# Two expert teams and one overflow team woven step by step, with gathers of 384 columns, in a two-block model on one core

## The reference

```python
def hierarchical_moe(h, w_group, b_group, w_router, b_router, w1, w3, w2):
    ...
    top_v, top_i = lax.top_k(e_in_group, TOP_K)
    top_w = jax.nn.softmax(top_v, axis=-1) * g_w
    ...
    hid = jax.nn.silu(jnp.einsum('td,edf->tef', t, w1)) * jnp.einsum('td,edf->tef', t, w3)
    y = jnp.einsum('tef,efd->td', hid * gates.astype(hid.dtype)[:, :, None], w2)
```

## Time and profile before

| | us |
|---|---|
| median of three runs | 3269.16 |
| lowest and highest run | 3265.61, 3270.73 |
| the profiled execution | 3263.18 |
| its span | 3261.4 |

### The profile page before, as it was taken

One profiled execution on the slowest core, in us unless ns is written; L12 is line 12 of the kernel. 1 busy time (PEld: TensorE's weight loads), 2 busy tenths in 40 slices (PEclk: granted clock), 3 DMA queues, 4 the chain that ended last, 5 costly groups with the idle time before them and its releaser, 6 DMA issues.

```text
span 3261.4 us, 51720 instructions
## 1 busy us (share of the span) xinstructions
PE 2918.5 (89%) x20048; PEld 2413.4 (74%) x20048; DVE 1270.4 (39%) x2025; ACT 1183.5 (36%) x1378; POOL 1677.4 (51%) x1274
## 2 busy tenths in 40 slices
PE   6899979999899999857788768979999999999998
PEld 1677767787898878733344427879988989999998
DVE  1477742214363252331222214436633153324335
ACT  1222233333445332310111104546554446654343
POOL 0000047677677676400000003966669997769798
PEclk8999989999999999978999988989999999999999
DMA  9533337558344586659777893543335554445444
GB/s 390 205 109 109 109 112 287 199 217 296 133 151 158 182 305 249 223 209 414 328 321 314 333 420 148 191 140 138 132 131 193 182 195 155 154 142 193 158 168 142
DMA packets 98628, 679.77 MB, mean 208 GB/s; under 512 B 11584, under 2 KB 15424, under 8 KB 16832
## 3 DMA queue, kind: packets, MB, share of 16 engines
q1 hardware_dynamic: 83088, 602.97, 49.4%
q10 hardware_dynamic: 15408, 74.85, 6.1%
...
## 4 chain that ended last, share of the span: by engine, by line
PE 70%; DMA 12%; DVE 6%; ACT 5%; issue 3%; POOL 2%; ACTq 1%; SPq 1%; DVEq 0%; POOLq 0%
PE acc L567 42%; PE wk L567 11%; PE acc L640 9%; DMA ring<-in_moe 6%; PE acc L644 5%; DMA side_buf<-in_ada 3%; POOL w_lo L549 2%; DMA stage<-in_ada 2%; PE acc L653 2%; ACT L1287 1%; ACT w_hi L1287 1%; DVE C_z L1846 1%; DMA stage<-in_main 1%; SPq L499 1%; ACT hb L1287 0%
## 5 line engine op out<-in xcount | busy, mean ns | idle before, releaser
L549 POOL TENSOR_TENSOR w_lo<-stage,w_hi 128x512 fp32r<-128x512 f32 x1268 | 1670.2, 1351 | 1535.3 <-ACT w_hi L1287 1014.3
L1287 ACT ACTIVATE w_hi<-stage 128x2048 fp32r<-128x2048 f32 x317 | 603.8, 1907 | 47.9 <-DMA stage<-in_main 47.5
L567 PE MATMUL acc<-xhl,w_hi 128*128 128x256 f32 x4064 | 525.2, 288 | 21.9 <-DVE xhl L1843 9.8
L567 PEld LDWEIGHTS acc<-xhl,w_hi 128*128 128x128 f32 x4064 | 509.2, 196 | 25.9 <-DVE xhl L1843 6.8
L640 PE MATMUL acc<-xhl,w_hi 128*128 128x512 f32 x1536 | 371.3, 394 | 0.0
L640 PEld LDWEIGHTS acc<-xhl,w_hi 128*128 128x128 f32 x1536 | 281.6, 188 | 92.7 <-issue 37.7
L567 PE MATMUL acc<-xhl,w_lo 128*128 128x256 f32 x2032 | 274.6, 289 | 2.0 <-POOL w_lo L549 2.0
L567 PEld LDWEIGHTS acc<-xhl,w_lo 128*128 128x128 f32 x2032 | 259.3, 196 | 5.5 <-issue 2.5
L567 PE MATMUL acc<-h,stage 128*128 128x256 f32 x1024 | 232.8, 384 | 2.9 <-ACT h L1287 2.9
L567 PEld LDWEIGHTS acc<-h,stage 128*128 128x128 f32 x1024 | 193.5, 191 | 38.3 <-issue 12.8
L567 PE MATMUL acc<-ring,xg 128*32 128x512 f32 x1024 | 145.2, 712 | 73.0 <-DMA ring<-in_moe 72.3
...
## 6 DMA issues: line engine op xcount, KB each, us to landing
...
ring<-in_moe SPq DMA_DIRECT2D x192, 1024.0 KB, 10.4
...
```

Source lines behind the costliest of these rows:

```text
L549: last = pool.tensor_tensor(w_lo[:, k % 2, cs], stage[:, k, cs], w_hi[:, k, cs].bitcast(F32), ALU.subtract)
L567: return pe.matmul(o, w, r, start=start, stop=stop)
L1287: return act.activation(o, i, f, **kw)
```

## The change

The teams now come in four rounds of three: two real teams `a` and `b`, and one overflow team `o`. The loop over `p` gives way to a list that is the same in each round, in which each real step is followed by at most one or two pieces that take nothing from the ring: an overflow step, a combine, half a gather. The combines of `b` and `o` and the down steps of `o` move into the up steps of the next round's `a`. The chunks' order in `EXPERT` follows: `a` 0 to 3, `b` 0, `a` 4 and 5, `b` 1 to 5. There are four passes of `gather` with 384 columns, for three teams each, in place of six with 256; each but the first is done in two halves. The overflow team's picked tokens have a buffer of their own, `xgo`, so ScalarE empties each PSUM tile by two operations. `pg` and `pk2` move to other addresses. The numbers of matmuls per step, the bytes, and all that lies outside of the expert stage stay as they were.

```diff
-TEAM_ORDER = [0, 1, 2, 8, 3, 9, 4, 10, 5, 11, 6, 7]
+TEAM_ORDER = [0, 1, 8, 2, 3, 9, 4, 5, 10, 6, 7, 11]
...
-    for p, team in enumerate(TEAMS):
-        yield from ((tile, c) for c in range(4) for tile in team)
-        if p and p - 1 not in OVER_TEAMS:
-            yield from ((tile, c) for c in (4, 5) for tile in TEAMS[p - 1])
-        if p in OVER_TEAMS:
-            yield from ((tile, c) for c in (4, 5) for tile in team)
-    yield from ((tile, c) for c in (4, 5) for tile in TEAMS[-1])
+    for d in range(TRIPLES):
+        a, b, o = TEAMS[3 * d:3 * d + 3]
+        for team, chunks in ((a, range(4)), (b, (0,)), (a, (4, 5)), (b, (1, 2, 3, 4, 5)), (o, range(6))):
+            yield from ((tile, c) for c in chunks for tile in team)
...
-                 ("pk", [P, 2, T]), ("pk2", [P, 2, P]), ("g2", [P, 16]), ("gg", [P, 16])]:
+                 ("pk", [P, 2, 3 * P]), ("g2", [P, 16]), ("gg", [P, 16])]:
...
+    R["pk2"] = sb("R_pk2", [P, 2, P], at=OT)
+    R["pg"] = sb("R_pg", [P, 2, P], at=OT + 1024)
+    xgo = ar("xgo", [P, TEAM, DT, CAP])
...
-                     ("pick_at", [P, 2, GROUP * CAP], F32R)]:
+                     ("pick_at", [P, 2, 3 * P], F32R)]:
...
+        def gather(g, tiles):
+
             pe.wait_ge(pick_ready, g + 1)
-            if g == 1:
-                pe.wait_ge(gT_ready, 1)
-            for i in range(8):
-                n = g * 8 + i
-                bank = 2 + i % 2
+            for t in tiles:
+                n = g * DT + t
                 if n >= 2:
                     pe.wait_ge(xg_ready, n - 1)
-                for j in range(2):
-                    t = 2 * i + j
-                    o = acc[:, bank, j * T:(j + 1) * T]
-                    for h in range(2):
-                        mm(o, xt_hi[:, h, t * P:(t + 1) * P], pick_at[:, h, :], h == 0, False)
-                        last = mm(o, xt_lo[:, h, t * P:(t + 1) * P], pick_at[:, h, :], False, h == 1)
+                if g and t == 1:
+                    pe.wait_ge(gT_ready, 3 * g - 1)
+                if g and t == 9:
+                    pe.wait_ge(gT_ready, 3 * g)
+                for h in range(2):
+                    mm(acc[:, 3 - t % 2, 0:3 * P], xt_hi[:, h, t * P:(t + 1) * P], pick_at[:, h, :], h == 0, False)
+                    last = mm(acc[:, 3 - t % 2, 0:3 * P], xt_lo[:, h, t * P:(t + 1) * P], pick_at[:, h, :], False, h == 1)
                 last.then_inc(xg_done, 1)
...
                               w[a][:, j * 512:(j + 1) * 512], c == 0 and j == 0, c == 3 and j == 3)
             last.then_inc(taken(team[0], 0)[0], len(team))
...
-                pe.transpose(acc[:, turn_bank(p), c * P:c * P + rows], X["hid"][0:rows, c * P:(c + 1) * P], ident[0:rows, 0:rows])
+                pe.transpose(acc[:, 2, c * P:c * P + rows], X["hid"][0:rows, c * P:(c + 1) * P], ident[0:rows, 0:rows])
             pe.wait_ge(pg_ready, p + 1)
             for h in range(2):
-                last = pe.transpose(acc[0:rows, turn_bank(p), T + h * P:T + (h + 1) * P], X["pg"][:, h, 0:rows], ident[:])
+                last = pe.transpose(acc[0:rows, 2, T + h * P:T + (h + 1) * P], R["pg"][:, h, 0:rows], ident[:])
             last.then_inc(turn_done, 1)
...
-        gather(0)
-        for p in range(len(TEAMS)):
-            if p in OVER_TEAMS:
-                down(p - 1)
-                turn(p)
-                gather(p // 2 + 1)
-                combine(p - 1)
-                down(p)
-            else:
-                up(p)
-                if p % 2 and p // 2 + 1 < TILE_GROUPS:
-                    gather(p // 2 + 1)
-                if p and p - 1 not in OVER_TEAMS:
-                    down(p - 1)
-                turn(p)
-                if p:
-                    combine(p - 1)
-        down(len(TEAMS) - 1)
+        gather(0, range(DT))
+        for d in range(TRIPLES):
+            a, b, o = 3 * d, 3 * d + 1, 3 * d + 2
+            pe.wait_ge(xg_ready, DT * (d + 1))
+            if d:
+                pe.wait_ge(hid_ready, a - 1)
+            up_step(a, 0)
+            if d:
+                combine(b - 3)
+            up_step(a, 1)
+            if d:
+                down_step(o - 3, 0)
+            up_step(a, 2)
+            if d:
+                down_step(o - 3, 1)
+            up_step(a, 3)
+            if d:
+                combine(o - 3)
+            pe.wait_ge(hid_ready, a + 1)
+            up_step(b, 0)
+            turn(a)
+            up_step(o, 0)
+            down_step(a, 0)
+            down_step(a, 1)
+            up_step(b, 1)
+            up_step(o, 1)
+            combine(a)
+            up_step(b, 2)
+            up_step(o, 2)
+            up_step(b, 3)
+            up_step(o, 3)
+            turn(b)
+            if d + 1 < TRIPLES:
+                gather(d + 1, range(DT // 2))
+            down_step(b, 0)
+            down_step(b, 1)
+            turn(o)
+            if d + 1 < TRIPLES:
+                gather(d + 1, range(DT // 2, DT))
+        combine(len(TEAMS) - 2)
+        for c in range(2):
+            down_step(len(TEAMS) - 1, c)
         combine(len(TEAMS) - 1)
         for i in range(5, 8):
...
-        def rows_in(g):
-            for i in range(8):
-                act.wait_ge(xg_done, g * 8 + i + 1)
-                fn(xg[:, :, 2 * i:2 * i + 2, :].rearrange("p a t c -> p t a c"),
-                   acc[:, 2 + i % 2, :].rearrange("p (t a c) -> p t a c", t=2, a=GROUP), ACT.Copy).then_inc(xg_ready, 1)
+        def rows_in(g, tiles):
+            for t in tiles:
+                act.wait_ge(xg_done, g * DT + t + 1)
+                o = acc[:, 3 - t % 2, :].rearrange("p (a c) -> p a c", c=CAP)
+                fn(xg[:, :, t, :], o[:, 0:GROUP, :], ACT.Copy)
+                fn(xgo[:, :, t, :], o[:, GROUP:GROUP + TEAM, :], ACT.Copy).then_inc(xg_ready, 1)
...
-                over_load(d, 4)
-                rows_out(p - 1)
-                rows_in(p // 2 + 1)
-                over_load(d, 5)
-                rows_out(p)
-                if d + 1 < len(OVER_TEAMS):
-                    over_load(d + 1, 0)
-            else:
-                if p % 2 and p // 2 + 1 < TILE_GROUPS:
-                    rows_in(p // 2 + 1)
-                if p and p - 1 not in OVER_TEAMS:
-                    rows_out(p - 1)
+
+        for d in range(TRIPLES):
+            a, b, o = 3 * d, 3 * d + 1, 3 * d + 2
+            if d:
+                over_load(d - 1, 5)
+                over_load(d, 0)
+                rows_out(o - 3)
+            silu(a)
+            over_load(d, 1)
+            rows_out(a)
+            over_load(d, 2)
+            over_load(d, 3)
+            silu(b)
+            silu(o)
+            over_load(d, 4)
+            if d + 1 < TRIPLES:
+                rows_in(d + 1, range(DT // 2))
+            rows_out(b)
+            if d + 1 < TRIPLES:
+                rows_in(d + 1, range(DT // 2, DT))
+        over_load(TRIPLES - 1, 5)
         rows_out(len(TEAMS) - 1)
         for n in range(BASE["kv"], BASE["kv"] + 4):
             high(*slot(n))
...
         def pick_rows(g):
             if g:
-                dve.wait_ge(xg_done, 8 * g)
+                dve.wait_ge(xg_done, DT * g)
             for h in range(2):
-                for a in range(2):
-                    q = TEAM_ORDER[2 * g + a]
+                for a in range(3):
+                    q = TEAM_ORDER[3 * g + a]
                     ts(R["pk"][:, h, a * P:(a + 1) * P], R["iota"][:, 0:P], R["off"][:, 0, h, q:q + 1],
                        ALU.is_equal).then_inc(pick_half, 1)
             for h in range(2):
-                for a in range(2):
-                    q = TEAM_ORDER[2 * g + a]
...
         dve.wait_ge(mod_ready, 7)
-        for p, team in enumerate(TEAMS):
-            rows = CAP * len(team)
+        def hidden(p):
+            rows = CAP * len(TEAMS[p])
             dve.wait_ge(s_ready, p + 1)
             if p:
                 dve.wait_ge(turn_done, p)
             tt(X["hid"][0:rows, :], X["s"][0:rows, :], acc[0:rows, up_bank(p), T:2 * T], MUL).then_inc(hid_ready, 1)
-            more = p % 2 and p // 2 + 2 < TILE_GROUPS
-            if more and p not in OVER_TEAMS:
-                pick_rows(p // 2 + 2)
+
+        def turned(p):
+
+            rows = CAP * len(TEAMS[p])
             dve.wait_ge(turn_done, p + 1)
             if p:
                 dve.wait_ge(*taken(TEAMS[p - 1][-1], 5))
-            cp(X["hT"][:, :, 0:rows], acc[:, turn_bank(p), 0:T].rearrange("p (a b) -> p a b", a=2)[:, :, 0:rows]).then_inc(hT_ready, 1)
-            cp(X["gT"][0:rows, p % 2, :], acc[0:rows, turn_bank(p), T:2 * T]).then_inc(gT_ready, 1)
-            if more and p in OVER_TEAMS:
-                pick_rows(p // 2 + 2)
+            if p > 1:
+                dve.wait_ge(comb_done, 8 * (p - 1))
+            cp(X["hT"][:, :, 0:rows], acc[:, 2, 0:T].rearrange("p (a b) -> p a b", a=2)[:, :, 0:rows]).then_inc(hT_ready, 1)
+            cp(X["gT"][0:rows, p % 2, :], acc[0:rows, 2, T:2 * T]).then_inc(gT_ready, 1)
             if p + 1 < len(TEAMS):
```

(19 more changed lines are left out.)

79 lines of the change are left out of this document (32 added, 47 removed).

## The result

| | before | changed |
|---|---|---|
| median, us | 3268.67 | 3236.27 |
| lowest and highest run | 3265.61, 3270.73 | 3231.22, 3241.93 |
| span of the profiled execution | 3261.4 | 3229.4 |
| first ring step starts | 1424.81 | 1430.17 |
| last set of the ring lands | 1968.17 | 1914.57 |

The ratio is 0.9904, 95% interval 0.9889 to 0.9919: the changed kernel is faster by 32 us, where 39 were forecast.

The account below looks back on a forecast made before the run. Holes in the ring's transfers, not memory, bound the expert stage. 1433.8 + 2.6 + 462.3 + 10 = 1908.7, plus stretched step 5.15 and tail 18.7, gives 1932.6 against 1971.8: -39 us, 3230; range 3213 to 3257.

Parts of the forecast that it names:

- Holes, not memory, bound the ring: Expert stage: the ring stops while TensorE does work that takes no chunks; 75 us of the stage are holes.
- rival A: Expert stage: the ring really is as slow as its average, 358 GB/s; +26 us, 3295; chance 0.04.
- The head, +5.5: Before the ring's first free slot: longer first gather, more masks and sums make it 5.5 us later, at 1433.8.
- Start-up 2.6, then 10.05 a set: Ring transfers: 2.6 us to start into an empty ring, then 46 sets at 10.05 us, 462.3 in all.
- The weave's remaining loss, 10 us: Expert stage rounds: TensorE too late at two places still costs 3 us a round, 10 in all.
- the list: TensorE's work without ring chunks after each of a round's 12 ring steps, followed to find lateness beyond 5 us.
- The stretched last step, 5.15: Last ring step, after the last set lands: stretched to 5.15 us.
- The half gathers: Gathers of 384 columns done in halves mid-stage: 7.0 and 7.2 us, hidden under the transfers.
- The tail, +18.7: After the last ring step: copy, combine and two overflow steps add 18.7 us to the path, with no cover.
- Part four, the queues: ScalarE's queue: slow overflow loads ahead of a combine make it wait 0 to 1 us; other loads cost zero.
- B (lower clock): Work between ring steps runs at the lower clock: loss of 90 in place of 10, +41, 3310; chance 0.05.
- C (holes shrink but stay): Queue or bank delays TensorE 3 to 5 us more each round: loss 23 to 30, 3243 to 3255; chance 0.16.

Follow-up runs that it names:

- unwoven kernel: Changed kernel with the combine of b, the two down steps of o and the combine of o in a row before the next round's a0: 3334.9 us.
- The kernels of the table: The changed kernel and four variants with overflow steps moved or cut, or idle matmuls added, compared by lateness and loss in round one; medians 3222.3 to 3247.0 us.
- slack kernel: Changed kernel with 15 idle matmuls added after a4 and 15 after a5 in each round, where TensorE waits for the ring anyway: 3224.5 us.

## Why the prediction was right, and which term was off

By its own steps, with the profiled executions (-32.1 at the stage's end, where -39 was summed):

- **Holes, not memory, bound the ring.** Right. 402 GB/s over the stage; rival A (358 as the memory's own rate) is out, and the unwoven kernel brings holes and time back, 93 us at the three places.
- **The head, +5.5.** Right: the first gather begins 0.9 later after its masks and takes 14.9 in place of 10.4, +5.4. The first free slot came at 1430.17 + 3.45 = 1433.6, against 1433.8.
- **Start-up 2.6, then 10.05 a set.** Right for the start (1446.26 - 1433.6 - 9.93 = 2.7), and high for the pace: undisturbed sets land 9.93 apart. 46 sets took 481.0, against 474.9 with the 10 of loss in it. The pace gave 5.5 back, so the losses were larger than the difference of 6 shows; that the two errors cancel by half is luck.
- **The weave's remaining loss, 10 us.** This is the term that was mis-sized: it is 21.5 over 45 sets at 9.93. That TensorE comes late, and where, was right to some tenths in the first round: b2 5.9 late by the list and 5.7 measured (5.6 to 6.8 in the others), b3 2.7 and 2.7, b4 7.1 and 7.1. Wrong was the step "the ring holds one more set, so TensorE may begin 4.0 late, or 6.6; I take 5". The kernels of the table give about 2.5, below even the 4.0. It would follow from the same sum with a renewed instruction load in it: 9.93 - 3.45 - 2.6 - 1.3 = 2.6; that part is argued, the 2.5 is measured. At this allowance the four places at b2 lose 14.7. Another 4.6 go between b5 and the next a3: b4 starts 3.7 late against the landing of b5 (1534.16 and 1540.36 - 9.93), and in two of the three rounds a1 is 4.1 late, where the list had 2.4, since it had b5 at full speed and b5 took 5.34. The first jump is 1.4, and 0.8 is spread. The list also counted one thing twice: the 0.9 lost at b2 shift the ring, so b4's excess was 1.2 and not 2.1.
- **The stretched last step, 5.15.** It took 6.5, +1.3.
- **The half gathers.** The first took 1527.26 to 1534.16, 6.9 us with its wait of 0.2 for the transposed copy, where the list uses 7.0; the terms named for it, 6.2 and 0.3, make 6.5, so 0.5 of the 7.0 had no source. The second took 7.6 with the hand-over at its end, against 7.2.
- **The tail, +18.7.** 18.6: 10.2 to the first overflow step and 8.5 for the pair, as summed.
- **Part four, the queues.** Right as far as it goes: a combine behind the slow loads waited 1.37 us once (1712.02). The unwoven kernel shows what that delay costs without cover: 7.94 us of waiting, 6 more than for the copy alone.
- **Rivals.** B (lower clock) has a true core: steps after idle stretches took 5.0 to 6.6, and 1.2 to 2.5 us a round of the loss came from it, as the slack kernel shows. Its price of 41 didn't come, since the tight place of the first round, 1500 to 1540, runs at a granted clock of 0.98 to 1.00. C (holes shrink but stay) is nearest to what happened: the loss of 21.5 almost reaches its 23 to 30. But its cause is another: TensorE was hardly later than the list had it, the ring allowed it less.

Of the signs that were named, three spoke against the forecast. No window of 10 us should be under 300 GB/s, and 1510 to 1520 had 283. Low windows recur at b2, after each b1, which was named as the sign of being wrong on the weave; they are part of the loss of 21.5 us, small against the 75 us of holes. And TensorE's waits for the ring neither grew in number (22 after 25) nor shrank in length (4.1 us after 3.9 on average); they only shifted to the down steps.
